# Where GpSimd makes the adaptive-norm vectors of a two-layer decoder: moved from the projection stages into attention and the first feed-forward stage

## The reference

```python
for l in range(DEPTH):                                   # DEPTH = 2
    ada = silu(c) @ W_ada[l] + b_ada[l]                  # (1024) @ (1024, 6144)
    sh1, sc1, g1, sh2, sc2, g2 = split(ada, 6)           # six vectors of 1024
    u = x * (1 + sc1) + sh1
    x = LayerNorm(ALPHA * x + (1 + g1) * Mixer(u))       # attention in two forms
    u = x * (1 + sc2) + sh2
    x = LayerNorm(ALPHA * x + (1 + g2) * SwiGLU(u))      # width 2816
```

## Time and profile before

| What | Value |
|---|---|
| median of three runs | 1960.57 us |
| span of the profiled execution, first to last instruction | 1955.2 us |
| GpSimd busy, of which L544 and L543 | 380.0 us; 192.7 and 85.9 us |
| VectorE, ScalarE busy | 1013.1, 625.2 us |
| mean granted TensorE clock, share of full | 0.949 |
| chain of waits: TensorE, VectorE, ScalarE, DMA | 73%, 15%, 5%, 4% |

### The profile page before, as it was taken

How to read it: one execution, slowest core, us unless ns; L and a number is a source line. 1 busy time by engine, 2 the same in 40 slices (tenths; PEclk the granted TensorE clock), 3 DMA queues, 4 the chain that set the end, 5 groups by cost and what they waited for, 6 DMA issues and landing times.

```text
span 1955.2 us, 21770 instructions
## 1 busy us (share of the span) xinstructions
PE 1770.7 (91%) x8565; PEld 1427.8 (73%) x8565; DVE 1013.1 (52%) x1375; ACT 625.2 (32%) x1122; POOL 380.0 (19%) x274
## 2 busy tenths in 40 slices
PE   5789889999997999999967789899999899999997
PEld 5568766767775888888846677667777678888885
DVE  4973845555656434333377585555556643333334
ACT  1320234444525222222152022444443342222223
POOL 2653650000004514000055565000000020000000
PEclk8886999999998999999988689999999999999999
DMA  8444531001232534333324545110112223333331
GB/s 312 131 143 145 164 108 34 22 23 43 84 96 84 171 114 142 97 89 99 103 76 140 172 130 165 40 33 22 33 55 86 86 75 92 101 92 100 90 98 54
DMA packets 285972, 192.90 MB, mean 99 GB/s; under 512 B 8072, under 2 KB 272816, under 8 KB 284848
## 3 DMA queue, kind: packets, MB, share of 16 engines
q1 hardware_dynamic: 271920, 148.79, 25.9%
q0 software_dynamic: 12032, 42.07, 6.9%
q10 hardware_dynamic: 1920, 0.66, 0.1%
HBM read 189.39 MB, written 2.10 MB: 98 GB/s over the span
## 4 chain that ended last, share of the span: by engine, by line
PE 73%; DVE 15%; ACT 5%; DMA 4%; issue 3%; SPq 0%; DVEq 0%; ACTq 0%
PE banks L1365 20%; PE banks L1367 20%; PE banks L1366 20%; PE banks L1430 3%; DVE w_lo L856 3%; PE banks L1463 2%; PE banks L1488 2%; ACT probs L764 2%; PE banks L1549 2%; DVE t L935 1%; DVE kdT L939 1%; DMA ring<-in_cmp_w_k_dram 1%; DMA ring<-in_w_in_dram 1%; PE banks L1432 1%; DMA ada_first_a<-in_w_ada_dram 1%
## 5 line engine op out<-in xcount | busy, mean ns | idle before, releaser
L1365 PE MATMUL banks<-u_hi,w_hi 128*128 128x512 f32 x1328 | 550.7, 415 | 69.6 <-DVE w_lo L856 36.9
L1366 PE MATMUL banks<-u_lo,w_hi 128*128 128x512 f32 x1328 | 528.3, 398 | 0.0
L1367 PE MATMUL banks<-u_hi,w_lo 128*128 128x512 f32 x1328 | 528.0, 398 | 0.0
L856 DVE TENSOR_TENSOR w_lo<-ring,w_hi 128x1024 fp32r<-128x1024 f32 (+1 forms) x246 | 329.9, 1341 | 359.1 <-ACT w_hi L613 357.9
L613 ACT ACTIVATE w_hi<-ring 128x1024 fp32r<-128x1024 f32 (+1 forms) x246 | 255.2, 1039 | 345.7 <-PE banks L1367 234.0
L1365 PEld LDWEIGHTS banks<-u_hi,w_hi 128*128 128x128 f32 x1328 | 257.3, 194 | 124.2 <-DVE w_lo L856 40.8
L1367 PEld LDWEIGHTS banks<-u_hi,w_lo 128*128 128x128 f32 x1328 | 255.5, 192 | 55.9
L1366 PEld LDWEIGHTS banks<-u_lo,w_hi 128*128 128x128 f32 x1328 | 257.2, 194 | 44.9
L555 POOL TENSOR_SCALAR res<-yT,mul_r,add_r 128x512 f32<-128x512 f32 x24 | 32.2, 1347 | 913.5 <-DVE yT L978 913.5
L544 POOL TENSOR_TENSOR ada_acc<-ada_acc,ada_ring 128x1024 f32<-128x1024 f32 x70 | 192.7, 2753 | 6.2
L1367 PE MATMUL banks<-h_hi,w_lo 128*128 128x512 f32 x352 | 136.9, 389 | 0.0
(11 more groups left out here) (211 smaller groups left out, 2216.4 us busy)
## 6 DMA issues: line engine op xcount, KB each, us to landing
ring<-in_w_ffn_in_dram SPq DMA_DIRECT2D x88, 512.0 KB, 3.7
ada_ring<-in_w_ada_dram POOLq DMA_DIRECT2D x80, 512.0 KB, 4.1
ring<-in_w_in_dram SPq DMA_DIRECT2D x78, 512.0 KB, 3.6
ring<-in_w_ffn_out_dram SPq DMA_DIRECT2D x32, 448.0 KB, 3.6
ring<-in_w_out_dram SPq DMA_DIRECT2D x16, 512.0 KB, 3.7
ring<-in_w_ffn_out_dram SPq DMA_DIRECT2D x16, 512.0 KB, 3.7
ada_first_a<-in_w_ada_dram SPq DMA_DIRECT2D x5, 1024.0 KB, 9.1
ring<-in_cmp_w_k_dram SPq DMA_DIRECT2D x8, 512.0 KB, 4.6
```

The costliest lines, as they stand in the source:

```text
L856: V.tensor_tensor(lo, src, hi.bitcast(fp32), ALU.subtract).then_inc(split_lo, 1)
L1365: M(bank, wh[:, block], sh[:, k, :], start=start, stop=False)
L1366: M(bank, wh[:, block], sl[:, k, :], start=False, stop=False)
L1367: return M(bank, wl[:, block], sh[:, k, :], start=False, stop=stop)
```

## The change

The four sums of layer 0 (vectors 2 to 5) now stand in its attention, ahead of the gate chunks `gm4`, `gm6`, `gm8` and `gm10`, which are steps 19, 28, 37 and 47 of 56, counted from 0. All six sums of layer 1 stand in layer 0's feed-forward stage, ahead of `fa5`, `fa8`, `fa11`, `fa14`, `fa17` and `fa20`. Layer 1 has none. GpSimd waits for the first scores of layer 0 (`scored`) before its first group, and runs groups 4 to 9 in one go between the two residuals of layer 0. `gate1` gets one slot for each layer. The number of groups, slices and sums is the same, and so is every operation in them.

```diff
-ADA_BEFORE = {"qn1": 2, "kd1": 3, "vd1": 4, f"gm{GM_IN}": 5, "fa10": 0, "fa20": 1}
+FIRST_ADA = {"gm4": 2, "gm6": 3, "gm8": 4, "gm10": 5}
+NEXT_ADA = {"fa5": 0, "fa8": 1, "fa11": 2, "fa14": 3, "fa17": 4, "fa20": 5}
 def ada_before(l, name):
-    j = ADA_BEFORE.get(name)
-    if j is None or (j < 2 and l + 1 == DEPTH):
-        return None
-    return (l + 1 if j < 2 else l, j)
+    if l == 0 and name in FIRST_ADA:
+        return (0, FIRST_ADA[name])
+    if l + 1 < DEPTH and name in NEXT_ADA:
+        return (l + 1, NEXT_ADA[name])
+    return None
...
-        gate1 = sb("gate1", [P, 2, KD])
+        gate1 = sb("gate1", [P, DEPTH, 2, KD])
...
             pool.wait_ge(part1, 1)
+            pool.wait_ge(scored, 1)
             ada_groups(0, 4)
             for l in range(DEPTH):
                 residual(l, 0)
                 if l + 1 < DEPTH:
-                    ada_groups(4 + 6 * l, 6 + 6 * l)
+                    ada_groups(4 + 6 * l, 10 + 6 * l)
                     residual(l, 1)
-                    ada_groups(6 + 6 * l, 10 + 6 * l)
...
                             if k == 0:
                                 prepare_behind(l, f"gm{m}")
+                                save_ada(l, f"gm{m}")
...
-                save_ada(l, f"gm{GM_IN}")
                 ada_part2(l)
...
                 if k == 0:
+                    sum_ada(l, name)
                     take_split(l, name)
                     take_bank(l, name)
...
-                sum_ada(l, f"gm{GM_IN}")
```

More of the change, by code:

```diff
@@ L911, in save_ada @@
                 elif j in (2, 5):
-                    V.tensor_scalar(gate1[:, j // 3, :], ada[:, l, 8 * j:8 * j + 8], 1.0, None, ALU.add)
+                    V.tensor_scalar(gate1[:, l, j // 3, :], ada[:, l, 8 * j:8 * j + 8], 1.0, None, ALU.add)
                 V.memset(d_mix[:, 0:1], 0.0).then_inc(saved(l, f"ada{j}"), 1)
@@ L952, in layernorm @@
                         dve.wait_ge(res_ready, n * KD)
-                    V.scalar_tensor_tensor(yT[:, m, :], bank_of(l, names[m]), gate1[:, which, m:m + 1],
+                    V.scalar_tensor_tensor(yT[:, m, :], bank_of(l, names[m]), gate1[:, l, which, m:m + 1],
                                            res[:, m, :], ALU.mult, ALU.add).then_inc(saved(l, names[m]), 1)
@@ L1069, in _ @@
                 for i in range(4):
-                    save_ada(l, f"qn{i}")
                     prepare_behind(l, f"qn{i}")
@@ L1091, in _ @@
                     for i in range(4):
-                        save_ada(l, f"{a}{i}")
                         prepare_behind(l, f"{a}{i}")
@@ L1096, in _ @@
                 for i in range(4):
-                    save_ada(l, f"vd{i}")
                     prepare_behind(l, f"vd{i}")
@@ L1536, in _ @@
                 for i in range(4):
-                    sum_ada(l, f"qn{i}")
                     project(l, f"qn{i}")
@@ L1567, in _ @@
                 for name in [f"{a}{i}" for a in ("kd", "qd") for i in range(4)]:
-                    sum_ada(l, name)
                     project(l, name)
                 for i in range(4):
-                    sum_ada(l, f"vd{i}")
                     project(l, f"vd{i}")
```

## The result

The kernel after took 1938.57 us, the median of four runs (1934.61 to 1941.04), against 1961.3 us for the kernel before (four runs, 1959.1 to 1963.83): a ratio of 0.9882 [0.9866, 0.9897], so 1.2% less. The forecast was 1921 in a range of 1900 to 1946. The sign and the range were right. The gain is 22.7 us, where 39 was forecast.

The account below looks back on a forecast made before the run. TensorE, busy 91%, bounds the kernel; time is won only where it stands still or runs at the low clock. 1955.2 - 85 (gains) + 24.5 (attention) + 21.8 (feed-forward) = 1916.5 span, median 5.4 above: 1921 us, range 1900 to 1946.

Parts of the forecast that it names:

- third rival: Projection stages not freed to 5.44 us a chunk, because something takes the place of `w_lo`: 1947 us; chance 0.12.
- (a): Layer 1's input projection, `ksl` to `hk`: nine chunks at 5.44 us, transposes and VectorE; 79.3 to 52.0 us, gain 27.
- (b): Layer 1's compression net: of 8.4 us of waits for its weights about 1.5 stay, gain 6.5 us.
- (c): Layer 1, `kd0` to `vd3`: 81.9 us down to 68.6, gain 13.3 us.
- (d): Layer 1's attention: no sum ahead of `gm12` (1.9 us) and about 1 us of port waits gone, gain 3 us.
- Gain, layer 0: Layer 0 ahead of attention: `kc` to `hk` 18 us, compression net 6, `kd0` to the end 11; together 35.
- port waits on VectorE: Layer 0's attention: 45 VectorE instructions with two SBUF inputs wait for GpSimd, 0.74 us each, 33 us.
- 60% on the path: Share of the 33 us of VectorE waits that lengthens layer 0's attention: 20 us, less 1 there before, so 19.
- fourth rival: VectorE becomes the bound of layer 0's attention by the port: 2001 us, slower; decides from 1.28 us an instruction; chance 0.06.
- Near miss: Layer 0's attention: `gm6` comes some 38 to 39 us after `gm4`, GpSimd needs 37; 1 us of cost.
- Feed-forward: Layer 0's feed-forward stage: four more sums 7.2 us, five TensorE waits for GpSimd's groups 14.6; cost 21.8 us.
- first case: Everything as summed: 1921 us, chance 0.68; with its waits varied, 1903 to 1944.

Follow-up runs that it names:

- Section 2: Kernel after, with GpSimd's multiplies and adds in layer 0's four attention groups replaced by constant writes that read nothing: 1900.9 us, ratio 0.97.
- section 3: Kernel of Section 2 with 29 extra VectorE products of 128x512 in layer 0's attention: 1932.5 us, ratio 0.9861.
- section 1: Kernel after with only one layer's sums moved, the other's as before: layer 1's alone 1934.9 us (0.9883), layer 0's alone 1964.1 us (1.0022).
- section 4: Kernel after with a second accumulator for GpSimd's groups in layer 0's feed-forward stage: 1937.6 us, ratio 0.9872.
- section 6: Kernel after with layer 1's six sums at every fourth chunk pair instead of every third, the last behind `fo1`: 1921.9 us, ratio 0.9798.
- the quarters: Kernel after with GpSimd's multiplies and adds in attention's groups cut in four: 1938.4 us, ratio 0.9892; with later sums as well, 1915.6 us, 0.9769.

## Why the prediction was right, and where it failed

**Price of a chunk, 5.44 us, and that layer 1's projection would reach it: right.** `w_lo` every 5.44 us, 52.4 us against 52.0 predicted. The third rival (projection not freed, 1947) is out.

**Gain, layer 1, 50 predicted, 53.5 measured.** (a) 26.8 for 27. (b) the compression net 9.2 for 6.5: its waits for those loads fell from 8.4 us to 2.3, about as forecast. The rest is the clock, which I had left out: the first 16 of its narrow matmuls took 3.65 us before and 1.89 after. (c) 14.1 for 13.3. (d) 3.3 for 3.

**Gain, layer 0, 35 predicted, 39.1 measured:** 21.8 for 18, 7.0 for 6, 10.3 for 11. VectorE's setup copies cost nothing where I had put 4.

**Attention, port waits on VectorE, 33 us: the sum nearly right, its parts not.** 27.5 measured. Of the kinds counted 19 instructions waited, not 45, and 1.24 us each, not 0.74; 4.0 us come from a kind that wasn't counted. L1117, the L1118 of before, which was forecast to be longer, never waited in this profile.

**"I put 60% on the path": this step failed.** It gave 19 us, the stage shows 42.5 beside the sums (49.7 - 7.2). Section 2 shows that 38 of them go when GpSimd stops reading SBUF, and section 3 that a microsecond of VectorE here costs 1.3, not 0.6. In a step of attention scores, maximum, exponential, transposes and values follow one another with one buffer of scores, so the 2 to 3 us that VectorE idles are no reserve: they are the time the others need for their links of the same chain. And around the stalls that follow TensorE's clock is 0.80 to 0.88, which the forecast didn't price at all. The 15 us that neither the sums (7.2) nor the waits (27.5) explain I put down to it; that split is a remainder, not a measurement, and 4 us of it stay in section 2, where hardly anything waits for the port. What the fourth rival feared came about in part: 42.5 / 45 = 0.94 us of path an instruction, under its 1.28. As a whole change it stayed faster, but layer 0's half alone is slower than before (section 1).

**Near miss, 1 us: not seen.** The groups were done at 258.5, 323.9, 371.5 and 420.1, the sums stood at 287.7, 335.4, 385.1 and 438.8. The longer steps of attention gave them the room.

**Feed-forward, 21.8 predicted, 29.6 measured.** Five waits came, as forecast, but of 1.1 to 5.3 us instead of 2.2 to 3.1, 10.8 us in all for 14.6; the four sums 7.2. The other 11.6 fit the clock, left out again: 0.96 over the 395 us, against 0.99 over the 366 before. The forecast took a group's 34.4 us as fixed by its place behind the sum; it wasn't (34.3 to 39.3), and the sum's turn on the shared accumulator was not what made the waits, as section 4 shows. Sums every fourth pair, which I had not thought of, take the cost away (section 6).

So both errors are one: a wait was priced by its own length. The gain in the projection was priced by stage lengths, with the clock in them, and came out right.

That the time still lies in the range is luck. The range allowed attention's waits 10 to 35 us, and they took 42.5; it held because its upper end, 1946, was drawn for the third rival, and because the gains were 7.6 us above the forecast; without them the time would stand at its edge. The stated upper end of the first case, 1944, isn't the sum of its own bounds either: 1921 + 15.4 + 16 is 1952.

## What to carry to other kernels

Before moving a second engine's work under another stage, ask of that stage whether its engines form a chain in which each waits for the last; if so, price every microsecond of delay at about one, and at 1.3 to 1.5 where single delays reach 0.7 us and more, though each engine is half idle. These factors are of this attention alone. Price a wait by the stretch around it, the granted clock included, not by its own row. Then choose the place by the room it gives (four chunk pairs rather than three), and where an engine must be disturbed, cut the disturbing instruction short and give the longer work a later due time.

## What the runs showed of the hardware

GpSimd's instructions have a cost that doesn't shrink with their width: 128x256 took 758 and 536 ns in the mean with their waits, 720 and 480 at the least, 128x1024 2.40 and 1.12 us. VectorE's wait did shrink with them, from 1.25 us to 0.30. By the Trainium skill (SBUF — State Buffer, "SBUF: two separate sides") whichever engine starts first holds the shared ports for its whole instruction; the quarters agree, with L1185 down from 687 to 270 ns. So do the 22 waits of the kernel after: 20 of these instructions started while GpSimd's ran, and the short ones ended within 0.03 us of its end.

A kind of instruction that I hadn't counted waited as well, products with one SBUF input, beside GpSimd's work. VectorE's groups by form, attention of layer 0, kernel after:

```profile
L911 DVE TENSOR_SCALAR ada<-ada 128x8 f32<-128x8 f32 x1 | 2.1, 2133 | 0.0
...
L1179 DVE TENSOR_SCALAR coef<-coef,cst 128x8 f32<-128x8 f32 x1 | 1.5, 1531 | 0.0
```

Without GpSimd, in layer 1's attention, L1179 took 0.23 us; the instruction of L911 took 0.17 in the kernel before. A third, L914, took 0.90 us once and 0.17 once. All three long ones ended within 0.03 us of the end of GpSimd's instruction. Beside the writes of section 2 L911's still took 0.58. Three instructions are few: that this form queues for the port is likely, not shown.
